# Attention value tiles turned into rows by way of device memory and VectorE instead of on TensorE

## What is computed

```python
aq, ak, av, mq, mk, mv, mi, mf, mo = split_in(xn @ w_in)
aq = rms_norm(aq.reshape(B, T, H_ATT, 2, DQK_ATT), q_norm_g)
ak = rms_norm(ak.reshape(B, T, H_ATT, 2, DQK_ATT), k_norm_g)
av = av.reshape(B, T, H_ATT, DV_ATT)          # 4 heads x 256
...
s = jnp.einsum('bqhcd,bkhcd->bchqk', q, k) * (DQK_ATT ** -0.5) + bias
p = jax.nn.softmax(s, axis=-1)
w = p[:, 0] - lam * p[:, 1]
o = jnp.einsum('bhqk,bkhd->bqhd', w, v)
```

## Time and profile before

| | us |
|---|---|
| median of 3 runs | 1741.83 (1741.75 to 1742.34) |
| span of the profiled execution | 1739.3 |
| TensorE busy | 1732.4 (100%) |
| VectorE busy | 915.0 (53%) |
| ScalarE busy | 665.3 (38%) |
| GpSimd busy | 374.7 (22%) |

### The profile page before, as it was taken

How to read it: one execution, slowest core, us unless ns; L and a number is a source line. 1 busy time by engine, 2 the same in 40 slices (tenths; PEclk the granted TensorE clock), 3 DMA queues, 4 the chain that set the end, 5 groups by cost and what they waited for, 6 DMA issues and landing times.

```text
span 1739.3 us, 24767 instructions
## 1 busy us (share of the span) xinstructions
PE 1732.4 (100%) x8460; PEld 1471.3 (85%) x8460; DVE 915.0 (53%) x1739; ACT 665.3 (38%) x1256; POOL 374.7 (22%) x531
## 2 busy tenths in 40 slices
PE   9999999999999999999999999999999999999999
PEld 8999998899997788888888888888888888888887
DVE  5634776666677655554343564343455334456333
ACT  5323754444354445333333333333333333333332
POOL 3301010002252251334000243100234100144100
PEclk9999999999999999999999999999999999999999
DMA  7675469998789575565444566444556434555543
GB/s 194 185 179 151 122 160 227 204 210 209 200 253 271 146 205 176 166 181 176 132 122 132 158 175 188 126 128 122 167 163 180 144 124 129 158 168 169 172 144 97
DMA packets 294064, 291.84 MB, mean 168 GB/s; under 512 B 96397, under 2 KB 201037, under 8 KB 293965
## 3 DMA queue, kind: packets, MB, share of 16 engines
q1 hardware_dynamic: 254886, 222.09, 46.2%
q0 software_dynamic: 24016, 64.58, 13.8%
q10 hardware_dynamic: 15062, 3.86, 1.1%
HBM read 259.84 MB, written 36.40 MB: 170 GB/s over the span
## 4 chain that ended last, share of the span: by engine, by line
PE 98%; DVE 1%; issue 0%; ACT 0%; POOL 0%; POOLq 0%; DVEq 0%; ACTq 0%
PE bank L671 9%; PE bank L672 9%; PE bank L625 9%; PE bank L626 9%; PE bank L624 9%; PE bank L670 9%; PE acc L525 8%; PE acc L526 8%; PE acc L527 8%; PE bank L2010 3%; PE ssb L670 2%; PE ssb L624 2%; PE ssb L671 2%; PE ssb L625 2%; PE ssb L672 2%; PE ssb L626 2%
## 5 line engine op out<-in xcount | busy, mean ns | idle before, releaser
L505 DVE TENSOR_TENSOR w_lo<-raw,w_hi 128x512 fp32r<-128x512 f32 x768 | 537.5, 705 | 750.9 <-ACT w_hi L496 750.4
L496 ACT ACTIVATE w_hi<-raw 128x512 fp32r<-128x512 f32 x768 | 482.6, 631 | 948.3 <-PE ssb L672 180.4
L525 PE MATMUL acc<-a_hi,w_hi 128*128 128x400 f32 (+1 forms) x768 | 268.1, 349 | 0.2 <-DVE w_lo L505 0.2
L526 PE MATMUL acc<-a_lo,w_hi 128*128 128x400 f32 (+1 forms) x768 | 263.0, 342 | 0.0
L527 PE MATMUL acc<-a_hi,w_lo 128*128 128x400 f32 (+1 forms) x768 | 262.3, 342 | 0.0
L671 PE MATMUL bank<-w_lo,a_hi 128*128 128x512 f32 x640 | 253.0, 395 | 0.0
L672 PE MATMUL bank<-w_hi,a_lo 128*128 128x512 f32 x640 | 252.6, 395 | 0.0
L625 PE MATMUL bank<-w_lo,x2g_hi 128*128 128x512 f32 x640 | 252.3, 394 | 0.0
L626 PE MATMUL bank<-w_hi,x2g_lo 128*128 128x512 f32 x640 | 252.2, 394 | 0.0
L624 PE MATMUL bank<-w_hi,x2g_hi 128*128 128x512 f32 x640 | 252.1, 394 | 0.0
L670 PE MATMUL bank<-w_hi,a_hi 128*128 128x512 f32 x640 | 252.1, 394 | 0.0
(11 more groups left out here) (352 smaller groups left out, 1831.0 us busy)
## 6 DMA issues: line engine op xcount, KB each, us to landing
raw<-in_w_up SPq DMA_DIRECT2D x128, 512.0 KB, 3.8
raw<-in_w_down SPq DMA_DIRECT2D x128, 512.0 KB, 3.8
raw<-in_w_in SPq DMA_DIRECT2D x94, 512.0 KB, 4.6
raw<-in_w_out SPq DMA_DIRECT2D x32, 512.0 KB, 4.9
u_turned<-m POOLq DMA_DIRECT2D x192, 64.0 KB, 3.0
stage<-u_turned POOLq DMA_DIRECT2D x16, 768.0 KB, 6.1
vc<-in_cache_v POOLq DMA_DIRECT2D x32, 256.0 KB, 6.9
kc<-in_cache_k SPq DMA_DIRECT2D x128, 64.0 KB, 3.2
```

The lines of the kernel that those rows point to most:

```text
L496: e.activation(w_hi[:, q], raw[:, slot, 4 * (q % 2):4 * (q % 2) + 4, :], ACT.Copy).then_inc(hi_ready, 1)
L505: e.tensor_tensor(w_lo[:, q], raw[:, slot, 4 * (q % 2):4 * (q % 2) + 4, :], w_hi[:, q].bitcast(F32), ALU.subtract).then_inc(lo_ready, 1)
L525: e.matmul(out, w_hi[:, q, kk], hi[:, k, at], start=k == 0, stop=False, skip_group_check=True)
L526: e.matmul(out, w_hi[:, q, kk], lo[:, k, at], start=False, stop=False, skip_group_check=True)
```

## The change

The eight value tiles no longer pass TensorE. SP stores a finished tile to device memory (`av_d`, 128 rows of 400), and loads it again into a new buffer `av_blk` so that each 32x32 block lies where VectorE's block turn makes rows of it. That takes 13 loads for a tile: for each of the four groups of 32 partitions, three of 32x4x32 (128 pieces of 128 bytes), and one of 32x4x16 for the last 16 prompt tokens. VectorE then turns the buffer with two instructions into `av_rows`.

- SP: value tile `n` is stored behind the loads of weight tile `n + 19` (`av_out`, waits for `acc_free`), and its 13 loads stand behind those of weight tile `n + 20` (`av_back`; they wait for the store and, as there is one buffer, for the turn of tile `n - 1`). Tiles 18 to 23 leave the register loop of SP for that and are written out.
- VectorE: `turn_av` comes after the second quarter, not the first; for tiles 6 and 7 the slots are 1 and 5.
- TensorE: its four transposes a tile are gone, and the PSUM banks of the value tiles are not used for them.
- GpSimd clears the unused part of `av_blk` once and waits for VectorE's eighth turn before it stores `av_rows`.
- Two semaphores are merged with others (`ones_r_made` into `consts`, `z_set` into `st_set`).

```diff
-    plan += [(4 * (j - AV_AHEAD), "av", j) for j in range(AV_AHEAD, 8)] + [(4 * j + 1, "ko", j) for j in range(8)]
+    plan += [(4 * (j - AV_AHEAD) + 1, "av", j) for j in range(AV_AHEAD, 8)] + [(4 * j + 1, "ko", j) for j in range(8)]
...
+        av_d = nc.dram_tensor("av_d", [8, P, TOK], F32).ap()
...
+            av_blk = sb("av_blk", [P, 4, 4, 32], scope=s)
...
-            read_out(e, *[("av", j) for j in range(8)])
+            e.wait_ge(S("av_turned"), 8)
...
-            with e.Fori(1, T_M // 2) as p:
+            with e.Fori(1, T_AV // 2 + 1) as p:
...
+            def av_out(n):
+
+                if 0 <= n < 8:
+                    e.wait_ge(acc_free, T_AV + n + 1)
+                    e.dma_start(av_d[n], m1[:, n]).then_inc(S("av_out"), 16)
+
+            def av_back(n):
+
+                if 0 <= n < 8:
+                    e.wait_ge(S("av_out"), 16 * (n + 1))
+                    if n:
+                        e.wait_ge(S("av_turned"), n)
+                    else:
+                        e.wait_ge(S("av_padded"), 2)
+                    at = n * P * TOK
+                    for j in range(4):
+                        rows = slice(32 * j, 32 * j + 32)
+                        for r in range(3):
+                            e.dma_start(av_blk[rows, r], bass.AP(tensor=av_d.tensor, offset=at + STARTS[r] + 32 * j,
+                                                                 ap=[[TOK, 32], [32 * TOK, 4], [1, 32]])).then_inc(S("av_in"), 16)
+                    e.dma_start(av_blk[0:32, 3, :, 0:TAIL], bass.AP(tensor=av_d.tensor, offset=at + STARTS[3],
+                                                                    ap=[[TOK, 32], [32 * TOK, 4], [1, TAIL]])).then_inc(S("av_in"), 16)
...
+            for t in range(T_AV + 2, T_M):
+                load_tile(e, t // 2, t % 2, w_in[0], 0, P * t)
+                av_back(t - 4 - T_AV)
+                av_out(t - 3 - T_AV)
...
                 load_tile(e, t // 2, t % 2, w_in[0], 0, col, behind=behind_load(t))
+                av_back(t - 4 - T_AV)
+                av_out(t - 3 - T_AV)
                 spill(t - 3)
...
-                if q == 0 and u >= 2:
-                    take_av(u - 2)
+                if q == 1 and u >= 2:
+                    turn_av(u - 2)
...
+            def turn_av(n):
+
                 cs = slice(n * P, (n + 1) * P)
-                e.tensor_copy(av_rows[:, 0:3, cs], b[:, 0:3 * P].rearrange("p (r n) -> p r n", n=P))
-                taken(e.tensor_copy(av_rows[0:TAIL, 3, cs], b[0:TAIL, 3 * P:4 * P]), ("av", n))
+                e.wait_ge(S("av_in"), 16 * 13 * (n + 1))
+                e.transpose(av_rows[0:32, 3, cs], av_blk[0:32, 3].rearrange("p i t -> p (i t)"))
+                e.transpose(av_rows[:, 0:3, cs],
+                            av_blk[:, 0:3].rearrange("p r i t -> p r (i t)")).then_inc(S("av_turned"), 1)
...
-                if q == 0 and u >= 2:
-                    turn_av(u - 2)
-                elif q == 1:
+                if q == 1:
```

More of the change, by code:

```diff
@@ L233, in plan_banks @@
     for t in range(T_AV, T_M):
-        if t >= T_AV + 2:
-            u.add(("av", t - T_AV - 2), (2, 4)[t % 2])
         for x in range(2):
@@ L238, in plan_banks @@
     for _, what, n in ATT_PLAN:
-        if what == "av":
-            u.add(("av", n), (2, 4)[n % 2])
-        elif what == "scores":
+        if what == "scores":
             u.add(("s", STEPS[n], 0), 2)
@@ L715, in _ @@
             e.memset(gw[:].bitcast(F32), 0.0).then_inc(S("gw_padded"), 1)
-            e.tensor_copy(ones_r[:], ones[:]).then_inc(S("ones_r_made"), 1)
+            e.tensor_copy(ones_r[:], ones[:]).then_inc(S("consts"), 1)
             e.wait_ge(S("x_in3"), 16 * X_PIECES[3])
@@ L779, in _ @@
             e.memset(av_rows[:, 3], 0.0).then_inc(S("av_padded"), 1)
+            e.memset(av_blk[0:32, 3, :, TAIL:32], 0.0).then_inc(S("av_padded"), 1)
             for n in range(16):
@@ L1341, in _ @@
             e.memset(eps_col[:], EPS).then_inc(S("st_set"), 1)
-            e.memset(zt[:, 0:8, 0:META], 0.0).then_inc(S("z_set"), 1)
+            e.memset(zt[:, 0:8, 0:META], 0.0).then_inc(S("st_set"), 1)
             b = take(e, "g1")
@@ L1541, in n_low @@
                    ALU.subtract).then_inc(S("n_low"), 1)
-            def take_av(n):
-                b = take(e, ("av", n))
+            def turn_av(n):
                 cs = slice(n * P, (n + 1) * P)
-                e.tensor_copy(av_rows[:, 0:3, cs], b[:, 0:3 * P].rearrange("p (r n) -> p r n", n=P))
-                taken(e.tensor_copy(av_rows[0:TAIL, 3, cs], b[0:TAIL, 3 * P:4 * P]), ("av", n))
+                e.wait_ge(S("av_in"), 16 * 13 * (n + 1))
+                e.transpose(av_rows[0:32, 3, cs], av_blk[0:32, 3].rearrange("p i t -> p (i t)"))
+                e.transpose(av_rows[:, 0:3, cs],
+                            av_blk[:, 0:3].rearrange("p r i t -> p r (i t)")).then_inc(S("av_turned"), 1)
             e.wait_ge(acc_free, T_AV)
@@ L1552, in _ @@
             read_out(e, "gcols")
-            e.wait_ge(S("av_padded"), 1)
+            e.wait_ge(S("av_padded"), 2)
             n_low(0)
@@ L1621, in att_work @@
                     if what == "av":
-                        take_av(n)
+                        turn_av(n)
                     elif what == "ko":
@@ L2096, in qk_sums @@
                 u = t - T_AV
-                if q == 0 and u >= 2:
-                    turn_av(u - 2)
-                elif q == 1:
+                if q == 1:
                     if u == 0:
-                        e.wait_ge(S("ones_r_made"), 1)
+                        e.wait_ge(S("consts"), 4)
                     e.wait_ge(S("n_low"), u + 1)
@@ L2173, in att_work @@
                     yield slot
-                    if what == "av":
-                        turn_av(n)
-                    elif what == "scores":
+                    if what == "scores":
                         e.wait_ge(S("n_done"), 8)
```

3 lines of the change are left out of this document (removed).

## The result

Before 1741.83 us, after 1772.38 us (medians of 5 runs each; 1771.4 to 1775.5 after). The ratio is 1.0177, 95% interval 1.0165 to 1.0189: 30.5 us slower, inside the range of 1747 to 1778 and 14.5 us above the 1757.9 that the sum gave. The profiled execution spans 1771.3 us, against 1739.3. Lines of the code have moved: `w_lo` is made in L503, `w_hi` in L494, the products are L523 to L525, SP stores a value tile in L946 and loads it back in L960 and L962, keys are loaded in L985, VectorE turns a value tile in L1575 and L1576, new keys in L1658, old keys in L1676.

The account below looks back on a forecast made before the run. TensorE, busy for all of the span, was taken as the bound. Waits behind SP's loads, net of the saved turns, added 16.1 us to 1739.3, giving 1755.4; the runs' 2.5 us offset made 1757.9, range 1747 to 1778.

Parts of the forecast that it names:

- last quarter of tile 24: On VectorE, it ends at 252.7 us instead of 246.05.
- What goes: Four turns on TensorE cost 0.44 us a set; eight sets, 3.5 us on the path, are saved.
- The ring: Tiles 0 to 5: SP's loads and VectorE's last quarter wait on each other, 11.2 us per tile against 9.49, six times.
- rival (d): Issues of 0.58 us or landings near 5 add up over six ring turns: some 1775 us (1768 to 1793); 15%.
- Tile 6: Its loads stand behind 16 key loads on SP; third quarter of tile 25 at 272.2, not 256.37: loss 15.8 us.
- Tile 7: VectorE's third quarter behind its turn is done at 283.7, TensorE there at 283.0: 16.1 us late at the end.
- The weights at nothing: Weight loads on SP move later by up to 13 issues: nothing, or up to 2 us if stream 1's keys come late.
- GpSimd and the bytes at nothing: GpSimd's later value stores cost nothing; 200 KB out and back per tile, some 40 GB/s on top of 131, nothing.
- The low end: Issues 0.355, landing 2.1, keys 0.53 us: ring 10.1, A = 245.9, in all +4 us, 1746.
- A: End of the last quarter of tile 24 on VectorE, forecast 252.7 us; times for tile 6 are counted from it.
- rival e: TensorE idles some 12 us before tile 25's third quarter; its clock falls to 1.2 GHz, adding 2 to 6 us, 1762; 17%.
- The rule on batching: The skill advises batching transfers; the 13 loads at 0.68 us each, one after another, give an estimated +43 us in all.

Follow-up runs that it names:

- padding run: Changed kernel with nine more short products at the very start of TensorE's program, nothing else changed: 1768.8 us (1.0154).
- version with six tiles by memory: Changed kernel, stream 0's keys on GpSimd, VectorE's turn behind the next tile's last quarter, tiles 6 and 7 turned on TensorE: 1740.4 us (0.9991).
- last order experiment: Changed kernel with VectorE's ko turns put before the turns of value tiles 6 and 7: 1771.8 us (1.0170).
- traffic-only run: Kernel before, TensorE's turns kept, with all added stores and loads on SP that VectorE never waits for: 1752.5 us (1.0060).
- run with both edits: Changed kernel with stream 0's key loads on GpSimd and VectorE's turn behind the next tile's last quarter: 1747.5 us (1.0041).

## Why the prediction was right, and where not

The sign, the two mechanisms and the place were right: most of the loss is VectorE's wait for loads behind SP's issues, in a ring for tiles 0 to 5, with the key loads ahead for tile 6. The amount was half of what came. By its own steps, in us:

| step | forecast | measured | from |
|---|---|---|---|
| last quarter of tile 24 | +6.6 (252.7) | +10.0 (256.09) | VectorE rows |
| tile 6, up to third quarter of tile 25 | +9.2 | +10.2 | 276.53 |
| tile 7, up to tile 26 | +0.3 | +7.0 | 292.58 |
| code | none | +3.6 | padding run |
| sum | +16.1 | +30.8 | 30.5 measured |

The first three rows are from the profiled executions, which differ by 32.0 us, the fourth from medians, so that the sum comes within 0.3 us of 30.5 is in part luck.

- **What goes.** 0.44 us a set was right: the version with six tiles by memory is 2.1 us ahead at the start of tile 23, behind five sets, which would be 2.2. In the changed kernel it was all lost behind the waits.
- **The ring.** The pitch is (256.09 - 186.28) / 6 = 11.6 us where I had 11.2, which with the last turn without `n_low` was to give a mean of 11.0. The term that failed is the issues: 12 x 0.40 = 4.8 was 5.8 to 6.8. I took 0.40, near the duration of single issues of other shapes, as the spacing; the rows below give a duration of 0.432 as the median, and from 245.91 to 251.70 are 12 intervals of 0.48. Landings made up for a part: 2.1 to 3.1 with the wake, 2.4 in the mean, against 2.8. The rival (d) with 0.58 an issue was too dear in this stretch.
- **Tile 6.** The key loads took 253.13 to 266.92, 13.8 us, forecast 13.5. The step was right within 1 us, and what is over is the issues again, 5.7 us for 4.8.
- **Tile 7.** This is the step that failed. I followed VectorE's queue behind the turn only as far as a key turn and the third quarter (283.7), and took for granted that TensorE wants a quarter next. It wants the scores of stream 0 first, which need four key turns, as they do in the kernel before; the last three and two quarters stand behind tile 7's turn, 4.9 us from 285.80 to 290.69. Nor is the late ScalarE the price, as the last order experiment shows: two chains end within 2 us of each other.
- **The weights at nothing.** Right in this kernel, but by luck: TensorE was 20 us late by then. With the wait gone the 16 key loads and 13 issues ahead of weight tile 27 cost 10.9 us, where I had allowed 2 at the most.
- **GpSimd and the bytes at nothing.** Right: 1.0002 with all the bytes and no wait, and in the changed kernel nothing is lost from 293 to 1200 us, where GpSimd's stores are later.
- **The low end.** Its A should be 246.1 (186.46 + 60.6 - 0.95), not 245.9; it changes nothing.
- **The clock (rival e).** The mechanism came: behind 11.27 us of idle time the granted clock of the stretch is 0.79, and the third quarter of tile 25 takes 276.53 to 280.21 = 3.7 us from its first product's start to its last's instead of 1.9, with a granted clock of 0.50 from 276.5 to 280.3, the lower of the two levels (1.2 instead of 2.4 GHz). The Trainium skill, TensorE: Matmul & The Clock Gate, Part 1, says that an idle TensorE falls to half its clock, and this agrees. But the price of 2 to 6 us did not come: TensorE then waited 2.8 us for `wT` and for the key turn anyway, so its slow quarters lay under that wait. It comes where no such wait follows: some 2.8 us in the traffic-only run, 1.5 in the run with both edits. In the changed kernel the clock was whole again from 282.2 to 285.8 (1.00) and fell a second time behind the 2.8 us of waiting (0.59 and 0.57 up to 292.6). On the path that leaves the scores of stream 0, 292.58 - 290.79 = 1.8 us instead of 265.37 - 264.32 = 1.05: 0.7 us.
- **The rule on batching.** The change is slower, as the rule would have it, but not for the bytes: by +30.5 us with the waits and by nothing without. The estimate of +43 us that I had made from the figure of the Trainium skill, DMA: Bandwidth & Descriptors, section Bandwidth (0.68 us for 4 KB), took the transfers one after another; the rows give 0.48 us from issue to issue and landings of 1.7 to 3.8, so several are in flight.
- **Not in any list:** TensorE's code. Taking 32 turns and their 32 weight loads out moved all of it that stands behind them.

The row and the wait that I had listed beforehand came: `av_blk<-av_d` in front of the 32x128 turn, 42.3 us in 8 waits (the first six 3.7 to 5.2 each, not 3; the seventh 13.5). By tile, after:

```profile
L960 SPq DMA_DIRECT2D av_blk<-av_d x96: 312/432/1442, 186.8 to 283.6; - x96
...
  DMA av_blk<-av_d: 42.3, 8
...
DMA to landing us min/median/max: 1.7/2.4/3.8
```

## What to carry to other kernels

Price a set of small DMAs by the number of issues times their spacing on the queue (0.48 us here, whether 64 or 128 pieces, and 0.8 while the DMA engines were full), then ask what stands behind them on that queue and behind the first wait for them on the engine that waits; put that wait behind what the bottleneck needs next. Follow the waiting engine's queue until the bottleneck's next instruction of every kind is served, not only the kind that one is looking at. And when an edit changes the number of instructions of the bottleneck engine by a few dozen, a difference of 0.2% can be the place of its code: pad the program and measure again before explaining it.

## What the runs showed of the hardware that I had not expected

- An issue on SP costs the same for half the pieces: 25 loads of 64 pieces stood 0.49 us apart, 13 of 128 pieces 0.48. While the DMA engines were full (share 1.08 and 1.09) the same issue took 0.76 to 0.81 us, in one run with key loads in flight and in the other without.
- 200 KB per value tile out in rows and back in pieces of 128 bytes, eight times, cost nothing measurable (1742.0 against 1741.7 us).
- Nine short products at the start of the program, with the same columns, made a kernel 4.3 us faster (1747.5 to 1743.2); a stall of 2.2 us, 1200 us later, beside a code transfer, disappeared with it and is a part of that.
- The clock dips in the ring's stretch (0.95 in both windows) show no cost: over the dip to 0.66 from 210 to 215 the ring took 11.66 us, and 11.2 to 12.6 in its other full turns.
- The halved clock behind an idle stretch cost only what no later wait covered: nothing behind 11.3 us of idle time, but 0.7 us behind 2.8, 1.5 behind 2.4 and some 2.8 behind 8.1.
